# Gate and output projections as three rounded products, output gating inside the delta rule, and a layer norm behind each tile, in a two-layer hybrid decoder kernel

## The reference, cut to what matters

```python
def gated_deltanet(x, w_in, ...):
    proj = x @ w_in                       # q, k, v, the gate z, and a, b
    qkv = causal_dwconv_silu(qkv, conv_w)
    ...
    o = chunk_gated_delta_rule(q, k, v, g, beta)
    o = rms_norm(o, onorm_w) * silu(z)
    return o.reshape(B, L, D_VA) @ w_out
...
h = layer_norm(DN_ALPHA * h + mix, ln1_g[layer], ln1_b[layer])
h = layer_norm(DN_ALPHA * h + moe_ffn(h, ...), ln2_g[layer], ln2_b[layer])
```

## Time and profile before

| | us |
|---|---|
| median of three runs | 2343.12 |
| the profiled execution, its own time | 2354.55 |
| its span in the trace | 2352.8 |
| PE busy | 2170.8 (92%) |
| DVE busy | 1507.8 (64%) |
| ACT busy | 1269.3 (54%) |
| POOL busy | 478.3 (20%) |

### The profile page before, as it was taken

The page is one execution under the profiler, slowest core; times in us unless marked ns, Lnnn a source line. Parts: engine busy times, 40 slices in busy tenths (PEclk is TensorE's granted clock), DMA queues, the critical chain, the costliest instruction groups (busy, mean ns, idle before and its releaser), DMA issues. The chain is left out here.

```text
span 2352.8 us, 35874 instructions
## 1 busy us (share of the span) xinstructions
PE 2170.8 (92%) x10145; PEld 1659.2 (71%) x10145; DVE 1507.8 (64%) x2488; ACT 1269.3 (54%) x2095; POOL 478.3 (20%) x369
## 2 busy tenths in 40 slices
PE   7999799979999999999996799999999999999993
PEld 6877789967577767777774656586667776777772
DVE  3761455455688877887874313526777777888884
ACT  3332233223377777777774222313577777777772
POOL 0000355300122222222221300000122222222220
PEclk9999899988999999999998797898999999999996
DMA  5221000003599999999998110015899999999993
GB/s 192 96 90 36 23 2 1 1 20 150 209 376 371 366 354 358 371 361 361 368 346 273 58 66 20 1 53 190 295 353 359 355 357 342 365 365 372 373 362 113
DMA packets 180098, 536.65 MB, mean 228 GB/s; under 512 B 26192, under 2 KB 57904, under 8 KB 180016
## 3 DMA queue, kind: packets, MB, share of 16 engines
q1 hardware_dynamic: 149824, 457.51, 51.5%
q0 software_dynamic: 25248, 69.25, 11.7%
q10 hardware_dynamic: 4944, 8.84, 1.0%
HBM read 501.57 MB, written 54.07 MB: 236 GB/s over the span
## 5 line engine op out<-in xcount | busy, mean ns | idle before, releaser
L1542 DVE TENSOR_TENSOR gu_l<-ring,gu_h 128x1024 fp32r<-128x1024 f32 x512 | 611.2, 1220 | 91.1 <-ACT gu_h L1428 88.9
L1428 ACT CAST gu_h<-ring 128x1024 fp32r<-128x1024 f32 x512 | 523.7, 1059 | 82.0 <-DMA ring<-in_moe_w_up 68.1
L1360 PE MATMUL bank<-gu_h,xgT_l 128*128 128x512 f32 x1024 | 414.4, 405 | 0.0
L1362 PE MATMUL bank<-gu_h,xgT_h 128*128 128x512 f32 x1024 | 402.4, 393 | 0.0
L1361 PE MATMUL bank<-gu_l,xgT_h 128*128 128x512 f32 x1024 | 401.8, 392 | 0.0
L1670 POOL DMA_INDIRECT xg<-h_rows,list_idx x128 | 146.1, 1142 | 908.1 <-issue 422.6
L1399 PE MATMUL bank<-ring,hmT_f 128*128 128x512 f32 x544 | 280.2, 596 | 0.0
L1435 ACT CAST down_h<-ring 128x1024 fp32r<-128x1024 f32 x130 | 136.2, 1047 | 228.0 <-DMA ring<-in_moe_w_down 126.1
L1689 POOL DMA_INDIRECT moe_sum<-y,out_idx x128 | 195.8, 1530 | 171.3 <-issue 152.8
L1548 DVE TENSOR_TENSOR down_l<-ring,down_h 128x1024 fp32r<-128x1024 f32 x130 | 159.4, 1226 | 109.7 <-ACT down_h L1435 109.2
L1362 PEld LDWEIGHTS bank<-gu_h,xgT_h 128*128 128x128 f32 x1024 | 193.9, 189 | 42.9
(11 more groups left out here) (318 smaller groups left out, 3338.7 us busy)
## 6 DMA issues: line engine op xcount, KB each, us to landing
ring<-in_moe_w_gate SPq DMA_DIRECT2D x256, 512.0 KB, 9.7
ring<-in_moe_w_up SPq DMA_DIRECT2D x256, 512.0 KB, 19.9
ring<-in_moe_w_down SPq DMA_DIRECT2D x256, 512.0 KB, 15.7
ring<-in_a_w_in SPq DMA_DIRECT2D x32, 512.0 KB, 5.2
ring<-in_a_w_out SPq DMA_DIRECT2D x8, 512.0 KB, 4.0
h_rows<-ring ACTq DMA_DIRECT2D x8, 512.0 KB, 2.6
moe_sum<-y ACTq DMA_DIRECT2D x8, 512.0 KB, 6.7
ring<-moe_sum SPq DMA_DIRECT2D x8, 512.0 KB, 5.2
```

The costliest lines, as they stand in the source:

```text
L1360: nc.tensor.matmul(out, lhsT=xl, rhs=wh, start=k == 0, stop=False)
L1362: last = nc.tensor.matmul(out, lhsT=xh, rhs=wh, start=False, stop=k == KD - 1)
L1428: nc.scalar.copy(gu_h[:, c, :, :], gate_up_cols(gate_slot, c * CH // 2, CH // 2)).then_inc(gu_hi.sem, 1)
L1542: nc.vector.tensor_tensor(gu_l[:, c, :, :], gate_up_cols(gate_slot, c * CH // 2, CH // 2), gu_h[:, c, :, :].bitcast(F32), ALU.subtract).th ...
```

## The change: what it does

1. The gate projection becomes three rounded products. It runs over 2 halves of 512 columns by 8 slices `k`. For each of these 16 steps ACT rounds 128x512 weights, DVE makes the remainder, and TensorE runs 3 matmuls of 512 columns for each of 4 tiles, which sum in 4 banks. The sums of squares stand behind steps 0 to 7. DVE copies 4 tiles of 512 columns once per half.
2. Gating moves from `gdn_out` into the delta rule for tiles 0 to 2: the squares of tile tt-1 stand behind level 1 of tile tt, one root for three tiles, the scale and the product with silu(z) in the last tile; silu(z) too is opened there. The weight `onorm` is a per-partition scale of the copies behind the transposes, and its broadcast DMA becomes a load of one column. The last chunk's state update, which nobody reads, is left out. Tile 3 is gated in `gdn_out`.
3. Both output projections become three rounded products over 2 halves of 512 columns per tile. The 16 slices of weights are split once, while tile 0 is multiplied; the remainder overwrites the weights in the ring. The first operand comes in two parts: in layer 0 the copies behind the transposes make them, in layer 1 ACT writes `attended_h` and DVE then `attended_l` in the attention loop.
4. In both output blocks the layer norm of a tile stands right behind its own sums, transposes follow one tile later, and the copy and store of rows stand behind the norm's root of the tile before.
5. POOL's 8 instructions on the residual move from `mla_projections` to `mla_attention`.

```diff
@@ gdn_projections: ACT, per step n
+            elif (n - 2) % KD == KD - 1:
+                act.wait_ge(z_ready.sem, z_ready.base + TT * ((n - 2) // KD + 1))
+            else:
+                act.wait_ge(z_used.sem, z_used.base + (n - 2) // KD * (KD - 1) + (n - 2) % KD + 1)
+            nc.scalar.copy(two_halves(z_parts(n)[0]), z_cols(n)).then_inc(qkv_w_hi.sem, 1)
...
-                for c in range(2 * H):
-                    if c >= 2:
-                        act.wait_ge(sums_ready.sem, sums_ready.base + c - 1)
-                    nc.scalar.activation(squares[:, c % 2, :], qkT[:, c, :], ACT.Square).then_inc(squared.sem, 1)
+                for n in range(4, 2 * KD):
+                    for c in range(2 * n - 6 if n > 4 else 0, min(2 * n - 4, 2 * H)):
+                        if c >= 2:
+                            act.wait_ge(sums_ready.sem, sums_ready.base + c - 1)
+                        nc.scalar.activation(squares[:, c % 2, :], qkT[:, c, :], ACT.Square).then_inc(squared.sem, 1)
+                    act_z_hi(act, n)
@@ gdn_projections: PE
+                for n in range(2 * KD):
+                    half, k = divmod(n, KD)
+                    pe.wait_ge(qkv_w_lo.sem, qkv_w_lo.base + 2 * N_QKV + n + 1)
+                    for tt in range(TT):
...
+                        nc.tensor.matmul(out, lhsT=hT_l[:, k, tok], rhs=wh, start=k == 0, stop=False)
+                        nc.tensor.matmul(out, lhsT=hT_h[:, k, tok], rhs=wl, start=False, stop=False)
+                        last = nc.tensor.matmul(out, lhsT=hT_h[:, k, tok], rhs=wh, start=False, stop=k == KD - 1)
...
+                    if n == 0:
+                        transpose_v(H - 1)
+                        pe.wait_ge(eps_set.sem, eps_set.base + 4)
                     if n < H:
                         sum_squares(2 * n)
                         sum_squares(2 * n + 1)
@@ gdn_delta_rule: ACT's decay, DVE
+                    if tt > 1:
+                        act.wait_ge(rms_in.sem, rms_in.base + tt - 1)
...
+                def out_squares(tt):
...
+                    for g in range(2):
+                        o, sq = v_tok[:, tt, HG * g:HG * g + HG, :], eg_row[g][:, :, :]
+                        link(v, "dve", nc.vector.tensor_tensor(sq, o, o, ALU.mult))
+                        link(v, "dve", nc.vector.tensor_reduce(o_rms[:, tt, HG * g:HG * g + HG], sq, AX.X, ALU.add))
+                    nc.vector.tensor_tensor(o_rms[:, tt, :], o_rms[:, tt, :], q_gain2[:, tt, :], ALU.mult).then_inc(rms_in.sem, 1)
...
+                        if level == 1 and tt > 0:
+                            out_squares(tt - 1)
+                        elif tt == TT - 1 and level == 3:
+                            v.wait_ge(rms_out.sem, rms_out.base + 1)
+                            dve_rms_gain(v, slice(0, TT - 1))
+                            dve_rms(v, 0)
+                        elif tt == TT - 1 and level == 4:
+                            dve_rms(v, 1)
+                            dve_gate(v, 0)
...
+                dve_gate(v, 1)
+                dve_rms(v, 2)
+                dve_gate(v, 2)
@@ mixer_out: PE
+                        for k in range(KD):
+                            m = KD * half + k
+                            if tt == 0:
+                                pe.wait_ge(w_lo_done.sem, w_lo_done.base + m + 1)
+                            wh, wl = w_high(m), w_low(m)
+                            nc.tensor.matmul(out, lhsT=mix_l[:, k, tok], rhs=wh, start=k == 0, stop=False)
+                            nc.tensor.matmul(out, lhsT=mix_h[:, k, tok], rhs=wl, start=False, stop=False)
+                            last = nc.tensor.matmul(out, lhsT=mix_h[:, k, tok], rhs=wh, start=False, stop=k == KD - 1)
@@ mixer_out: DVE
+                    for n in range(2 * KD):
+                        if gated and n == 2:
+                            dve_gated_lo(v, 0)
+                        w_lo(v, n)
...
+                            r = resid[:, tt, half * 512:(half + 1) * 512]
+                            nc.vector.scalar_tensor_tensor(out=r, in0=r, scalar=ALPHA, in1=bank[4 + n % 2][:, :], op0=ALU.mult, op1=ALU.add).then_inc(mixed_added.sem, 1)
+                            if gated and half == 0 and tt + 1 < TT:
+                                dve_gated_lo(v, tt + 1)
+                        v.wait_ge(mixed_added.sem, mixed_added.base + 2 * tt + 2)
+                        dve_layer_norm(v, tt, stats, gain, bias)
+                        if gated and tt == 0:
+                            dve_last_squares(v)
...
@@ mixer_out: ACT
                     for tt in range(TT):
                         if tt >= 1:
                             act_layer_norm(act, tt - 1, stats)
...
+                        if tt >= 1:
+                            act_rows(act, tt - 1)
+                            act_store_rows(act, tt - 1)
                     act_layer_norm(act, TT - 1, stats)
```

More of the change, by code:

```diff
@@ L140, in heads, with after @@
             return ap.rearrange("p (h q) -> p h q", q=P)
+        def after(c, n):
+            later = Count(c.sem)
+            later.base = c.base + n
+            return later
         slot_loaded = [sem(f"slot_loaded{i}") for i in range(SLOTS_IN_RING)]
@@ L543, in transpose_sums @@
                     for tt in range(TT):
-                        last = nc.tensor.transpose(bank[7][:, tt * P:(tt + 1) * P], sums[:, tt * P:(tt + 1) * P], ident)
+                        last = nc.tensor.transpose(bank[6][:, tt * P:(tt + 1) * P], sums[:, tt * P:(tt + 1) * P], ident)
                     last.then_inc(sums_ready.sem, 1)
@@ L986, in _ @@
                             first_X(2 * tt + 2 + c)
-                        for s in both(tt):
+                        for s in both(tt) if (tt, c) != (TT - 1, 1) else ():
                             _, g, _, b = tile(s)
@@ L1109, in _ @@
+                    for n in range(2 * TT):
+                        tt, half = divmod(n, 2)
+                        if gated and half == 0:
+                            pe.wait_ge(tr_copied.sem, tr_copied.base + 2 * tt + 2)
                         if n >= 2:
                             pe.wait_ge(mixed_added.sem, mixed_added.base + n - 1)
-                        w = unit_cols(u0 + u)
+                        out, tok = bank[4 + n % 2][:, :], slice(tt * P, (tt + 1) * P)
                         for k in range(KD):
-                            last = nc.tensor.matmul(bank[4 + n % 2][:, 0:256], lhsT=mixT[:, k, tt * P:(tt + 1) * P], rhs=w[:, k, :], start=k == 0, stop=k == KD - 1)
@@ L1707, in steps @@
                     step(eng, r, 0, True)
-            def after(c, n):
-                later = Count(c.sem)
-                later.base = c.base + n
-                return later
             if layer == 0:
@@ L2252, in _ @@
                 copy_rotated(act, 3)
-            @block.gpsimd
-            def _(pool):
-                for tt in range(TT):
-                    r = resid[:, tt, :]
-                    link(pool, "pool", nc.gpsimd.tensor_tensor(r, r, ln2_gain[0][:, :], ALU.mult))
-                    nc.gpsimd.tensor_tensor(r, r, ln2_bias[0][:, :], ALU.add).then_inc(resid_done.sem, 1)
             @block.vector
@@ L2342, in build, with _ @@
         with nc.Block(name="mla_attention") as block:
+            @block.gpsimd
+            def _(pool):
+                for tt in range(TT):
+                    r = resid[:, tt, :]
+                    link(pool, "pool", nc.gpsimd.tensor_tensor(r, r, ln2_gain[0][:, :], ALU.mult))
+                    nc.gpsimd.tensor_tensor(r, r, ln2_bias[0][:, :], ALU.add).then_inc(resid_done.sem, 1)
             @block.tensor
@@ L2378, in _, with copy_out_lo @@
             def _(v):
-                for n in range(NA + 1):
+                def copy_out_lo(n):
+                    qt, h = divmod(n, H)
+                    q = slice(qt * P, (qt + 1) * P)
+                    v.wait_ge(pv_hi.sem, pv_hi.base + n + 1)
+                    nc.vector.tensor_tensor(attended_l[:, h, q], bank[4 + n % 2][:, 0:P], attended_h[:, h, q].bitcast(F32), ALU.subtract).then_inc(pv_copied.sem, 1)
+                for n in range(NA + 4):
                     if n < NA:
@@ L2425, in _ @@
                         copy_out(n - 3)
-        nothing = lambda *_: None
-        mixer_out("mla_out", 1, attended, {"pe": nothing, "dve": nothing, "act": nothing, "act_copy": nothing, "pe_copied": nothing})
+        mixer_out("mla_out", 1, attended_h, attended_l, [kT_r, qT_r])
         att.close()
```

302 lines of the change are left out of this document (188 added, 114 removed).

## The result

The changed kernel takes 2329.98 us (median of 7 runs, 2324.75 to 2332.07) against 2343.12 (2338.48 to 2349.85), a ratio of 0.9941 [0.9919, 0.9963]. A second set of runs gave 0.9933 [0.9912, 0.9953]. All runs of the study together: 50 of before have a median of 2346.3, 13 of after 2330.0, so 16 us less (13 by the first set), where 26 were forecast.

The account below looks back on a forecast made before the run. TensorE was taken to bound the gate projection, attention and `mla_out`, with waits counting too in `gdn_out` and the delta rule's chain. -3.4 + 2.8 - 22.0 + 4.0 - 7.1 = -25.7 us from 2343.1 gives 2317; range 2298 to 2338.

Parts of the forecast that it names:

- Gate projection: Gate projection block: three rounded products per unit, less waits and low clock, -3.4 us; ends -10 and +5.
- more is won: Gate projection without waits (-6.6), output blocks without low clock (-4.3), attention without POOL holding DVE (-3.6): 2303 us; chance 0.15.
- The rival in which the clock stays low: Gate projection: waits keep TensorE at low clock; throughout +54.7 us, 2372, chance 0.06; through step 7 2346, sharing 0.14.
- Delta rule: Delta rule block: added squares and gating, less the dropped state update (1.1 back), +2.8 us; ends 0 and +9.
- tile 3's 2.0 us more beside POOL: Delta rule, tile 3: POOL works in DVE's gap, so products of two SBUF operands slow down, 2.0 us more.
- `gdn_out`: First output block: 94.0 to 72.0 us, products at 43.5, gating mostly moved out: -22.0 us; ends -27 and -10.
- At most 2.9 of tile 3's gating: `gdn_out`: DVE's work per tile, with at most 2.9 us of gating, is some 10 us beside TensorE's 13.
- The rival of 2345: Output blocks: in-order DVE holds the next sum behind a norm, norms not covered, 28 us back; shares chance 0.14.
- The splits: Tile 0 of output blocks: ACT and DVE alternate, 1.3 us a slice instead of 0.68, 2337; shares chance 0.15.
- Attention: Attention: POOL's instructions hold DVE's L2397 until they end (the lock); +4 us with 0.4 for remainders; ends 0, +19.
- `mla_out`: Second output block: 72.8 to 65.7 us, with 1.3 for an even chance of low clock: -7.1; ends -10, +5.
- the two expert blocks stay outside the sum: Expert blocks: 740 and some 742 us, unchanged, 0 in the sum; off 740 by more than 5 would show it wrong.

Follow-up runs that it names:

- the three orders: Changed kernel with squares ahead of the rounding, row copies behind the next norm's root, POOL's residual work back in the latent projections: 2311.34 us, ratio 0.9857.

## Why the forecast was right in its blocks and 13 us low in the time

By its own sum it was right: -25.7 us forecast, -25.6 in the same blocks. The closeness is luck: `gdn_out` gave 4.2 us less than forecast, the delta rule and the last two blocks 2.9 and 1.2 more, and these cancel.

- *Gate projection* (-3.4, measured -3.3). The waits of 1.3 us for ACT's order were there, 1.24 in the bracket. Their worth was put too low, at 6.6 under "more is won": without them the block ends 9.1 us earlier, and 7.7 in the trace of the three orders. The rival in which the clock stays low fell; the table of stretches of after reads 0.63 and then, through waits and sums, 1.00:

```profile
184.00:190.00 6.00, 6.00 (x15) 3.72 (x15) 0.00 (x0) 1.26 (x2) 0.00 (x0) 0.63 0.00 0
190.00:200.00 10.00, 8.76 (x31) 5.58 (x31) 0.69 (x1) 1.67 (x3) 0.00 (x0) 1.00 0.00 0
```

- *Delta rule* (+2.8, measured -0.1). The squares were counted at 3.9 us and cost 0.57, 0.57 and 0.52, 1.7 in all. The step that failed is tile 3's 2.0 us more beside POOL: of the 128x512 products only one grew, from 0.69 to 0.94. The dropped update, counted at 1.1 with the products at the end, gives 2.4 - 1.0 = 1.4. Together that is +0.3, and the measured -0.1 is the clock's: where the early low stretch lasts 13.7 us, before takes 223.5 and after 224.0 and 223.8.
- *`gdn_out`* (-22.0, measured -17.8). "At most 2.9 of tile 3's gating" was right as work, but not its place: behind a norm that waits for a copy on ACT. That is the missing step, 3.3 us: 1.9 of waiting and 1.4 of low clock. And "43.5 us" of products were 45.1, since here they come every 0.235 us, not 0.227: 1.6 us. The end of the block was as forecast, 13.04 us from the last sum to the next block instead of 11.58, for the wider sum and the copy ahead of the root.
- *Norms* ("while this cover holds, the norm costs nothing"): held; no sum of the residual made TensorE wait. The rival of 2345 fell.
- *The splits* fell as a rival too: in tile 0 TensorE's products come every 0.235 us once the clock is back.
- *Attention* (+4.0) and *`mla_out`* (-7.1): measured together -4.3 against -3.1. In the first traces the attention is 2.1 us longer and `mla_out` 6.7 shorter. By the eighth division the lock is worth 2.9 us and the remainders 0.2, so +4 was a little too large, and the lock, not the 0.4 without it, decided. The even chance of a low clock in `mla_out` came out in one of the two traces of after (64.7 and 63.1 us from its first product).

The number 2317 was made from the median of three runs, 2343.1, less the sum. The runs moved by 16 us, not 26. The step that failed is "the two expert blocks stay outside the sum", together with taking the sum from one trace to a median. Its sign of being wrong did appear: the second expert block took 747.2 us in the second trace of after. Of the 10 us, 4.1 are the expert blocks in the table, and 5.3 are that the three traces of before (2354.55, 2346.16, 2354.10, mean 2351.6) lie over its median of 2346.3, while those of after (mean 2330.0) lie on theirs. The record shows with what this excess goes, though not what causes it. For 43 of the 50 runs of before the mean granted clock is on record, and the time follows it (correlation -0.88): the six runs at 0.957 or less take 2350 us on average, the six at 0.962 or more 2337. The mean of the 43 is 0.959, while the three traces of before have 0.954, 0.959 and 0.956; the 13 runs of after have 0.957, and so have its two traces (0.959 and 0.955). So the traces of before caught more of the low clock than its typical run. Where in a typical run of before the clock stays high, no trace shows. The drops of the clock in the delta rule are a candidate on the side of after (2.6 us on average over the nine traces of changed code), longer expert blocks another (3.4 by the means); neither is shown, nor that the change causes them. The expert blocks keep the transfers busy for most of their time and scatter by 7 us with nothing changed; the forecast had them as a fixed 740 and 742.

## What to carry to other kernels

When a step is moved to be early, look at what stands behind it on its engine and has a due time; here a norm that nobody waited for delayed a gating for which TensorE waited. On an engine that serves several, put what others wait for (a root, a square, the first part of a split) ahead of work that nobody needs yet: two such orders, with POOL's work moved back to where it delayed nothing, were worth 19 us, more than the whole change. Compare changes block by block and over several traces, since a difference in the runs also holds the scatter of blocks that were not touched. And read a cost at the step where it arises, not only at the end of its block: at the eighth division the lock is 2.8 to 2.9 us in every trace, while the ends of the blocks, where the clock has its part, say 3.3 and 5.2.

## What was not expected of the hardware

A 128x512 product in float32r does not have one pace. At a granted clock of 1.00 products follow each other every 0.227 us in the q, k, v projection and every 0.230 to 0.235 in the output blocks; in the gate projection both are seen, so three of them take 0.68 to 0.70 us. The clock dropped in the same three places of the delta rule (76, 96 and 151 us after its start) in three traces and in none of them in others, with the same code in that block. And a drop of the clock does not need long idle time: 1.9 us of waiting ahead of tile 3's transposes went with one in four traces of five (0.57 from 516 to 520 us in the first trace of after).
